# A two-block transformer forward pass: the mLSTM half of the first mixer, its convolution moved behind the projections and its cell written as one step

## What is computed

```python
xc = jax.nn.silu(causal_conv(xm, conv_w, conv_b))          # 4 taps, 1024 features
q = heads(xc, wq); k = heads(xc, wk) * (Dh ** -0.5); v = heads(xm, wv)
dlog = jnp.where(causal, bcum[..., :, None] - bcum[..., None, :] + i_t[..., None, :], -jnp.inf)
m_t = jnp.maximum(bcum + m_prev_b, m_intra)
a_t = jnp.exp(bcum + m_prev_b - m_t)
qk = jnp.einsum('bhcld,bhcsd->bhcls', q, k) * jnp.exp(dlog - m_t[..., None])
num = a_t[..., None] * jnp.einsum('bhcld,cbhde->bhcle', q, c_prev) + jnp.einsum('bhcls,bhcse->bhcle', qk, v)
den = a_t * jnp.einsum('bhcld,cbhd->bhcl', q, n_prev) + jnp.sum(qk, axis=-1)
hid = num / jnp.maximum(jnp.abs(den), jnp.exp(-m_t))[..., None]
hid = head_rms_norm(hid, norm_w, H) * jax.nn.sigmoid(og.astype(F32))
```

## Time and profile before

| | before |
|---|---|
| median of 3 runs | 3710.71 us (3708.18 to 3719.13) |
| the profiled execution | 3716.57 us; its span 3714.8 us |
| PE, PE weight load busy | 81%, 63% of the span |
| DVE, ACT, POOL busy | 66%, 21%, 17% |
| DMA | 858.87 MB, mean 231 GB/s |
| mean granted TensorE clock | 0.899 |

### The profile page before, as it was taken

How to read it: one execution, slowest core, us unless ns; L and a number is a source line. 1 busy time by engine, 2 the same in 40 slices (tenths; PEclk the granted TensorE clock), 3 DMA queues, 4 the chain that set the end, 5 groups by cost and what they waited for, 6 DMA issues and landing times. The chain is left out here.

```text
span 3714.8 us, 45654 instructions
## 1 busy us (share of the span) xinstructions
PE 3005.0 (81%) x17504; PEld 2349.6 (63%) x17504; DVE 2464.5 (66%) x4579; ACT 777.1 (21%) x1927; POOL 633.9 (17%) x520
## 2 busy tenths in 40 slices
PE   7787796778786898677777779977878999975898
PEld 7576693333332598533333339976767999974798
DVE  5342467777777686777677758754446878765686
ACT  1213221222222232222222220012223001013300
POOL 0000003444445100254444520000000000000000
PEclk8899897988889899788988889977998999987999
DMA  6152358999999643799999966633213665640464
GB/s 204 59 169 67 114 166 325 415 411 408 415 410 421 235 136 117 284 415 415 415 406 409 419 286 178 191 103 100 83 35 109 178 190 161 188 151 6 121 182 152
DMA packets 469113, 858.87 MB, mean 231 GB/s; under 512 B 18720, under 2 KB 398496, under 8 KB 402464
## 3 DMA queue, kind: packets, MB, share of 16 engines
q0 software_dynamic: 73728, 536.90, 35.1%
q1 hardware_dynamic: 394880, 318.80, 28.1%
q10 hardware_dynamic: 288, 0.24, 0.0%
HBM read 848.55 MB, written 7.34 MB: 230 GB/s over the span
## 5 line engine op out<-in xcount | busy, mean ns | idle before, releaser
L2136 PE MATMUL banks<-arena,arena 128*128 128x512 f32 x1792 | 939.5, 683 | 344.2 <-ACT arena L2192 343.4
L2136 PEld LDWEIGHTS banks<-arena,arena 128*128 128x128 f32 x1792 | 381.6, 220 | 884.9 <-issue 454.7
L2096 POOL DMA_INDIRECT arena<-in_peer_uv,arena x512 | 628.9, 1228 | 1449.3 <-DVE arena L2278 759.5
L2301 DVE CUSTOM_DVE_ANT_0 arena<-arena,normed 128x1024 f32<-128x1024 f32 x512 | 626.5, 1224 | 260.3 <-DMA arena<-in_peer_uv,arena 258.0
L354 DVE TENSOR_TENSOR weight_ring_part<-weight_ring,weight_high_parts 128x2048 fp32r<-128x2048 f32 (+2 forms) x244 | 539.8, 2212 | 8.4
L2827 PE MATMUL banks<-normed_columns_part,weight_high_parts 128*128 128x256 f32 x1408 | 403.8, 287 | 10.7 <-PEq L302 9.0
L2828 PE MATMUL banks<-normed_part,weight_high_parts 128*128 128x256 f32 x1408 | 401.8, 285 | 0.0
L2829 PE MATMUL banks<-normed_columns_part,weight_ring_part 128*128 128x256 f32 x1408 | 401.8, 285 | 0.0
L663 PE MATMUL banks<-weight_high_parts,arena_part 128*128 128x256 f32 x1216 | 344.4, 283 | 42.5 <-PEq L302 28.9
L351 DVE CAST weight_high_parts<-weight_ring 128x2048 fp32r<-128x2048 f32 (+2 forms) x244 | 289.9, 1188 | 123.1 <-PE banks L665 79.6
L664 PE MATMUL banks<-weight_ring_part,arena_part 128*128 128x256 f32 x1216 | 341.6, 281 | 0.0
(11 more groups left out here) (506 smaller groups left out, 4357.7 us busy)
## 6 DMA issues: line engine op xcount, KB each, us to landing
weight_ring<-in_ffn_w_gate SPq DMA_DIRECT2D x88, 512.0 KB, 4.0
weight_ring<-in_ffn_w_up SPq DMA_DIRECT2D x88, 512.0 KB, 5.3
weight_ring<-in_ev_w_in SPq DMA_DIRECT2D x33, 1024.0 KB, 5.5
weight_ring<-in_ffn_w_down SPq DMA_DIRECT2D x32, 1024.0 KB, 5.3
weight_ring<-in_od_w_in SPq DMA_DIRECT2D x23, 1024.0 KB, 5.4
weight_ring<-in_xa_wkv SPq DMA_DIRECT2D x16, 1024.0 KB, 5.8
weight_ring<-in_peer_wq SPq DMA_DIRECT2D x16, 1024.0 KB, 5.7
weight_ring<-in_ev_w_out SPq DMA_DIRECT2D x12, 1024.0 KB, 5.7
```

Of the source, the lines that this page charges most:

```text
L2096: pool.indirect_dma_start(out=ring[:, slot(i, s), :], out_offset=None, in_=table, in_offset=bass.IndirectOffsetOnAxis(ap=index[:, i % 2, s ...
L2136: mm = pe.matmul(k.ps[:, 2 * b + half, :], diag[:, n % 2, s, :], v, start=h == 0 and g == 0 and s == 0, stop=h == PEER_HEADS - 1 and g == ...
L2301: dve.tensor_tensor_reduce(out=ring[:, here, 0:D], in0=ring[:, here, 0:D], in1=k.xn[:, b, :], scale=1.0, scalar=0.0, op0=ALU.mult, op1=ALU ...
```

## The change

1. `memory_columns` takes further pairs of gain and destination. In the SSD half's convolution step ACT evacuates each bank twice, with the first memory's gain into `memT` and with the second's into `memT_2`. The next step stores `memT_2` to memory (1 MB) and SP waits until it is stored. The second fetch of the memory rows and the second making of columns are gone; `memT` is fetched back (1 MB) during `rows_out`.
2. `zero_front` is an instruction of `columns_out` now. The 4-tap convolution is cut by chunk: chunks 0 and 1 between DVE's evacuations in `columns_out` (each instruction waits for the one before), chunks 2 to 7 between its weight splits in `rows_out`. The convolution step is gone.
3. Everything from Silu to the transposed output columns is one step, `mlstm`'s, with an order written out for each engine. The 32 side units stand at fixed places in PE's stream, `store_side` also feeds the weight ring after each, products run four banks ahead, and spread rows and scores are read by DVE out of PSUM. The sums with `spread` are fewer: `bcum` and the peak are applied as a bias of Exp and to row maxima. The root mean square is taken by ACT's Square for both chunks. Outputs are turned back chunk by chunk (`turn_out`), `finish_side` is gone.
4. The columns are written at once as rounded part `high` (ACT) and rest `low` (DVE, out of the bank), for the SSD half in its `to_columns`, for the mLSTM half in `keep_columns` and `keep_rest`. `split_columns` is gone. The split of the first two `ev_w_out` tiles stands on DVE between `keep_rest(0)` and `keep_rest(1)`.

```diff
+    def memory_columns(self, block, gain, rows, memT, *also):
...
+                for g, dst in ((gain, memT),) + also:
+                    act.activation(dst[:, m, :], self.ps[:, CHAIN + m % SIDE_BANKS, 0:T], ACT.Copy,
+                                   scale=self.col(g, m)).then_inc(self.memory_kept.sem, 1)
...
-    mixT = k.take(16, T)
+    columns = [k.take(16, T) for _ in range(2)]
+    high, low = (k.part_of(c) for c in columns)
...
+    k.conv(padded, "ssd_conv_w", "ssd_conv_b", 12, 4, xbcT, memory=("norm_mem0", memory_rows, memT, ("norm_mem1", memT_2)))
...
+        @block.sync
+        def _(sp):
+            sp.dma_start(k.kept_memory, memT_2).then_inc(k.memory_stored.sem, 16)
+            k.memory_stored.adds(16)
+            sp.wait_ge(k.memory_stored.sem, k.memory_stored.total)
...
-    k.to_columns(y, 8, mixT[:, 0:8, :], "ssd_norm")
...
+    k.to_columns(y, 8, None, "ssd_norm", parts=(high[:, 0:8], low[:, 0:8]))
     k.top = outer
+    mlstm(k, high, low, columns[1][:, 8:12].rearrange("p c t -> p (c t)"), gates, cum[:, :, 16:20], tot[:, :, 16:20], memT)
+    k.land((high, low), 16, "norm_xattn0")
...
-        k.fetch_memory_rows(sp, "mem", memory_rows)
-    zero_front(k, padded, 3)
+    def fetch_memory(sp):
+        sp.dma_start(memT, k.kept_memory).then_inc(k.fetched.sem, 16)
+        k.fetched.adds(16)
...
+    def clear_front(dve):
+        dve.memset(padded[:, :, 0:3], 0.0).then_inc(k.vector_done.sem, 1)
...
+    def convolve(dve, c):
+        for j in range(4):
+            x, w = padded[:, c, j:j + T], k.col("ml_conv_w", j * 8 + c)
+            if j == 0:
+                i = dve.tensor_scalar(xcT[:, c, :], x, w, k.col("ml_conv_b", c), ALU.mult, ALU.add)
+            else:
+                i = dve.scalar_tensor_tensor(xcT[:, c, :], x, w, xcT[:, c, :], ALU.mult, ALU.add)
+            i.then_inc(k.vector_done.sem, 1)
+            dve.wait_ge(k.vector_done.sem, k.vector_done.next())
...
+    def convolve_first(dve, m):
+        if m in (4, 6):
+            dve.wait_ge(k.evacuated.sem, k.evacuated.start + m - 3)
+            convolve(dve, m // 2 - 2)
+    def convolve_rest(dve, j):
+        for c in ((2, 3), (4,), (5,), (6, 7))[j]:
+            convolve(dve, c)
     k.columns_out(k.hT, [512] * 2, lambda e, m, bank: e.tensor_tensor(padded[:, m, 3:], bank, k.wide[:, :], ALU.mult),
-                  also=fetch_heads)
+                  also=fetch_heads, vector_first=clear_front, vector_then=convolve_first)
     k.rows_out(k.hT, [WIDTH] * 4, lambda e, j, b, bank: e.activation(og[:, b, j * WIDTH:(j + 1) * WIDTH], bank, ACT.Sigmoid,
-                                                                     scale=k.rs[:, b:b + 1]))
-    k.conv(padded, "ml_conv_w", "ml_conv_b", 8, 4, xcT, memory=("norm_mem1", memory_rows, memT))
+                                                                     scale=k.rs[:, b:b + 1]),
+               also=fetch_memory, vector_then=convolve_rest)
...
-    with k.step(side=2) as block:
...
+    with k.step() as block:
+        @block.sync
+        def _(sp):
+            k.feed(sp)
+            k.store_side(sp, range(s0, s0 + 16), feed=True)
+            k.feed(sp)
...
+            pe.wait_ge(k.heads_in.sem, k.heads_in.total)
+            for n in range(8):
+                project(n)
+            pe.wait_ge(k.ml_diag.sem, k.ml_diag.start + NB)
+            for b in range(NB):
+                pe.matmul(k.ps[:, 4 + b, :], k.c("ones"), diag[:, b].rearrange("p h s -> p (h s)"), start=True,
+                          stop=True).then_inc(k.ml_spread.sem, 1)
...
+            pe.wait_ge(k.ml_raised.sem, k.ml_raised.start + 8)
+            for n in range(8, 24):
+                project(n)
...
+            pe.wait_ge(k.fetched.sem, k.fetched.total)
+            k.multiply_side(pe, u0, u0 + 4)
...
+            pe.wait_ge(k.ml_kept.sem, k.ml_kept.start + 24)
+            for i in range(2):
+                for c in range(4):
...
+            for b in range(NB):
+                for h in range(H):
+                    for c in range(2):
+                        mm = pe.matmul(score_bank(b)[:, h, :], qT[:, 2 * h + c, b * P:(b + 1) * P], kT[:, 2 * h + c, b * P:(b + 1) * P],
+                                       start=c == 0, stop=c == 1)
...
+            k.multiply_side(pe, u0 + 4, u0 + 10)
...
+                pe.wait_ge(k.ml_weighted.sem, k.ml_weighted.start + b + 1)
+                for h in range(H):
+                    mm = pe.transpose(spread_bank(b)[:, h, :], shares[:, b, h, :], k.c("ident"))
+                mm.then_inc(k.ml_turned.sem, 1)
...
+            pe.wait_ge(k.ml_rows.sem, k.ml_rows.start + 2)
+            pe.wait_ge(k.ml_values.sem, k.ml_values.start + 1)
+            for n in range(8):
+                sums(n)
+                if n == 3:
+                    k.multiply_side(pe, u0 + 10, u0 + 12)
+            pe.wait_ge(k.ml_rows.sem, k.ml_rows.start + 4)
+            for n in range(8, 16):
+                sums(n)
+                if n == 11:
+                    k.multiply_side(pe, u0 + 12, u0 + 14)
+            for n in range(16, 20):
+                sums(n)
+            k.multiply_side(pe, u0 + 14, u0 + 24)
+            turn_out(0)
+            k.multiply_side(pe, u0 + 24, u0 + 32)
+            turn_out(1)
...
+            for c in range(8):
+                act.activation(xcT[:, c, :], xcT[:, c, :], ACT.Silu).then_inc(k.ml_raised.sem, 1)
+            for n in range(20):
+                keep(n)
+            act.wait_ge(k.ml_biased.sem, k.ml_biased.start + 2)
+            act.activation(w_end, w_end, ACT.Exp).then_inc(k.ml_raised.sem, 1)
...
+            k.keep_side(act, range(s0, s0 + 2))
+            keep_rows(0)
+            keep_rows(1)
+            k.keep_side(act, range(s0 + 2, s0 + 5))
+            keep_rows(2)
+            keep_rows(3)
+            for n in range(8):
+                keep_sums(n)
+            k.keep_side(act, range(s0 + 5, s0 + 6))
+            for n in range(8, 16):
+                keep_sums(n)
+            act.activation(k.spare, k.c("ones")[:, 0:1], ACT.Sqrt).then_inc(k.scalar_done.sem, 1)
+            k.keep_side(act, range(s0 + 6, s0 + 7))
+            square(0)
+            take_root(0)
+            k.keep_side(act, range(s0 + 7, s0 + 9))
+            square(1)
+            take_root(1)
+            k.keep_side(act, range(s0 + 9, s0 + 12))
+            keep_columns(0)
+            k.keep_side(act, range(s0 + 12, s0 + 16))
+            keep_columns(1)
...
+            def keep_rest(b):
+                dve.wait_ge(k.ml_high.sem, k.ml_high.start + 8 * (b + 1))
+                for m in range(8):
+                    t = slice(b * P, (b + 1) * P)
+                    dve.scalar_tensor_tensor(low[:, 8 + m, t], column_bank(b, m // 4)[:, m % 4, :], k.col("ml_norm", m),
+                                             high[:, 8 + m, t].bitcast(F32), ALU.mult, ALU.subtract).then_inc(k.columns_split.sem, 1)
...
+            divide(0)
+            mean(0)
+            for h in range(H):
+                dve.wait_ge(k.ml_summed.sem, k.ml_summed.start + 16 + h + 1)
+                dve.wait_ge(k.ml_sums.sem, k.ml_sums.start + 12 + h + 1)
+                step(dve.scalar_tensor_tensor(num[:, 1, h, :], k.ps[:, h, 0:DIM + 1], decay_prev[:, 1, h:h + 1], num[:, 1, h, :],
+                                              ALU.mult, ALU.add))
+            settled()
+            divide(1)
+            gate_out(0)
+            mean(1)
+            gate_out(1)
+            keep_rest(0)
+            while k.splits <= k.taken + 1:
+                k.split_next(dve, k.taken + 2)
+            keep_rest(1)
...
-    k.land(k.split_columns(mixT, k.take(16, T)), 16, "norm_xattn0")
```

More of the change, by code:

```diff
@@ L431, in _ @@
         def _(pe):
[L432 to L448 removed]
+            self.multiply_side(pe, first, last)
@@ L462, in finish_side, with keep_side @@
+    def keep_side(self, act, whole):
+        for s in whole:
+            act.wait_ge(self.side_done.sem, s + 1)
+            if s >= STAGES:
+                act.wait_ge(self.side_stored[s % STAGES].sem, 16 * (s // STAGES))
+            act.activation(self.stage[:, s % STAGES, :], self.ps[:, CHAIN + s % SIDE_BANKS, 0:WIDTH],
+                           ACT.Copy).then_inc(self.side_out.sem, 1)
+            self.side_out.adds(1)
     def finish_side(self):
@@ L1517, in even_mixer, with keep @@
-    with k.step() as block:
+            def keep(n):
+                act.wait_ge(k.ml_projected.sem, k.ml_projected.start + n + 1)
+                bank = k.ps[:, n % 4, 0:T]
+                if n < 8:
+                    act.activation(v_ext[:, n % 2, n // 2, 0:DIM], bank, ACT.Copy).then_inc(k.ml_kept.sem, 1)
+                else:
+                    is_key, m = chunk_of(n)
+                    act.activation((kT if is_key else qT)[:, m, :], bank, ACT.Copy,
+                                   scale=1.0 / 16 if is_key else 1.0).then_inc(k.ml_kept.sem, 1)
@@ L1588, in even_mixer @@
-    with k.step(side=1) as block:
-        @block.tensor
```

(27 more changed lines are left out.)

492 lines of the change are left out of this document (223 added, 269 removed).

## The result

| | before | after |
|---|---|---|
| median, beside each other | 3711.72 us (3708.18 to 3719.13, 4 runs) | 3668.49 us (3659.21 to 3676.47, 4 runs) |
| the profiled execution | 3716.57 us, span 3714.8 | 3664.38 us, span 3662.6 |
| mean granted TensorE clock | 0.899 | 0.905 |

The ratio is 0.9881, with a 95% interval of 0.9865 to 0.9897: faster by 43.2 us of the medians. The forecast was 3667.6 us.

The account below looks back on a forecast made before the run. No engine bounded the stretch; the order of steps did. The cell's 46.9 us less, minus costs of 2.7, 0.8 and 0.3, gave 43.1 us less: a median of 3667.6 us, range 3658 to 3682.

Parts of the forecast that it names:

- the cell: Silu to output columns as one step: 103.7 us to `land`'s first product instead of 150.6, so 46.9 us less.
- the clock rival: Rival, chance 0.04: PE's work in the cell runs at the lower clock level, +96 us over the whole step, 3763 us.
- The products of PE: In the cell: PE's products, priced by the distance of their evacuations, sum to 95.8 us at full clock.
- Ten hand-overs: In the cell: PE waits ten times for 0.15 us at hand-overs between engines, 1.5 us in all.
- Silu's wait: Start of the cell: the fifth v product waits for ACT's first kept bank, 0 to 1.2 us, taken as 1.0.
- The tail: Behind the cell's last transpose, uncovered: ACT's 8 copies 2.4 us, DVE's 8 rests 2.3 us, 0.1 us of hand-over.
- What was to be paid: Costs outside the cell: SSD half's `to_columns` +2.7 us, convolution in `columns_out` +0.8 us, in `rows_out` nothing.
- Second gain: SSD half's convolution step: 8 more copies on ACT end just behind DVE's taps, +0.3 us (0 to 0.5).
- The marks that were named: Signs in the changed kernel's profile, among them the first product of `columns_out` near 237.
- Hand-overs don't hide: Rival, chance 0.12: longer-held sums and changes between engines make the cell 15 us longer, 3683 us.
- The convolution isn't hidden: Rival, chance 0.04: at 2.4 us a chunk and more, `rows_out` gets longer by up to 4 us, 3672 us.
- The claim that `land` stays cold: Start of `land`: clock unchanged because PE is idle for 5.2 us before it; staying up would win some 2 us.

Follow-up runs that it names:

- e3: e2 with four of ACT's eight Silu chunks alternated with the first four kept banks: 3662.89 us, ratio 0.9864.
- e7: Changed kernel with all 32 side units in one run behind the projections instead of six portions: 3678.32 us, ratio 0.9925.
- e8: Changed kernel with three convolution chunks instead of two in the first tile of `rows_out`, one less in `columns_out`: 3662.18 us, one execution.
- e12: The changed kernel again, unaltered, on the same chip as e11: 3662.04 us, ratio 0.9882.
- e4: Kernel before with only the column halves changed (both `to_columns` write rounded part and rest, no `split_columns`): ratio 0.999.
- e6: Changed kernel with the convolution in a step of its own again: 3682.43 us, ratio 0.9931.
- e1: The changed kernel again, unaltered, beside e2 to e4: 3668.11 us, ratio 0.9877.
- e2: Changed kernel with the transposes of the outputs moved before the last side products: 3665.71 us, ratio 0.9872.
- e9: e3 with the SSD half's second split moved into `columns_out` and no fetch behind SP's last store: 3658.23 us, ratio 0.9859.
- e11: The kernel of e9 again, on a second chip: 3653.64 us, ratio 0.9871.
- e10: The changed kernel again, unaltered, on the same chip as e9: 3664.67 us, ratio 0.9874.

## Why the prediction was right, and where it was right by offset

**The total.** 43.1 us were forecast, 43.2 measured between the medians. That they agree to 0.1 is luck, since the ratio's interval reaches from 38 to 50 us. In the stretch it was less exact: -46.9 + 2.7 + 0.8 = -43.4 forecast, -45.4 measured, and another 0.3 forecast ahead of it. Two errors partly cancel there: the cell was 2.8 us shorter than forecast, and `columns_out` 1.1 us longer. (The chance of "faster" was also added up wrong: all but the clock rival, and half of that one, are 0.98 and not 0.96.)

**The products of PE: right.** The last transpose ends at 380.72 + 1.04 = 381.76; from 285.62 that is 96.14, less the wait of 0.44: 95.7 us against 95.8. Term by term it holds too, if less closely: the side products took 55.3 us (55.3 said), the sums 10.4 (10.4), q and k 13.8 (13.8), the scores 3.6 (3.8), the transposes 3.7 (3.9), v 7.25 without its wait (6.9). A single price can be read in e3, where no wait falls among the eight v products: 289.82 - 282.84 = 6.98 us, priced at 8 x 0.863 = 6.90. Pricing a product by the distance of its evacuations, in a stretch where PE doesn't wait, needs no model of the engine and was good to 0.4 us a term here and to 0.1 us in the sum.

**The waits: all too dear.** Ten hand-overs at 0.15 us, 1.5 us in all, measured nothing: PE's three idle lines above leave no room for one of that size. The portions of side work are longer than what each had to hide, and e7 shows that it is this, not that hand-overs are free. Silu's wait was taken at 1.0 us and is 0.44. The first bank was kept earlier, since ACT's lines are

```profile
285.58 1.28 ACT L1753 ACT_TABLE_LOAD   x1 [0.29 <-PEq L324]
286.87 2.56 ACT L1753 ACTIVATE arena<-arena 128x256 f32<-128x256 f32 x8
289.34 1.18 ACT L1714 ACTIVATE arena<-banks 128x256 f32<-128x256 f32 x4
```

and eight chunks take 2.56 us, between the 1.9 and 3.2 of the earlier trace rows; I took the upper end because the row was nearer by form. And Silu does need a table of its own. It starts 1.29 us after the load does: the drain that the Trainium skill adds to each switch ("ScalarE: Activation LUTs", section "What ACT_TABLE_LOAD costs") isn't seen here either, and the wait that would have been 1.4 us longer by it was shorter than forecast.

**The tail: right in kind, 0.5 us too long.** ACT 2.17 us, then DVE 2.16, said were 2.4 and 2.3; the change of step 0.3, said 0.4:

```profile
381.79 2.17 ACT L1750 ACTIVATE arena_part<-banks,feature_columns 128x128 fp32r<-128x128 f32 x8 [0.49 <-PE banks L1649]
...
384.00 2.16 DVE L1835 SCALAR_TENSOR_TENSOR arena_part<-banks,feature_columns,arena_part 128x128 fp32r<-128x128 f32 x8 [5.61 <-ACT arena_part L1750]
```

DVE's first rest waits for ACT's eighth copy, as foreseen. Together: hand-overs 1.5, Silu 0.56, tail and change 0.48, start 0.16, products 0.1 make 2.8 us, and the cell was 101.2 us where 104.0 was forecast from the same mark.

**What was to be paid.** `to_columns`: 2.5 us, said 2.7. `rows_out`: nothing, said nothing, and e8 put the point where it would cost at the place that the forecast named. The chunk itself was 1.97 us in the forecast; in the trace a chunk runs from 272.53 to 274.54 with the start of the next instruction:

```profile
272.53 0.41 DVE L1558 TENSOR_SCALAR arena<-arena,feature_columns 128x256 f32<-128x256 f32 x1
272.98 1.53 DVE L1560 SCALAR_TENSOR_TENSOR arena<-arena,feature_columns,arena 128x256 f32<-128x256 f32 x3
274.54 1.23 DVE L373 CAST weight_high_parts<-weight_ring 128x2048 fp32r<-128x2048 f32 x1
```

`columns_out` cost 1.9 us, said 0.8. Its own mechanism was right: the first of the two chunks costs nothing, since PE runs ahead, and the second moves the end, PE's idle time behind it going from 0.84 to 1.54 us: 0.7. The other 1.1 had no term in the sum. It is the clock in its first ten microseconds, here before, after and in e12:

```profile
234.20:244.20 10.00, 9.91 (x70) 9.94 (x71) 2.74 (x4) 0.00 (x0) 0.00 (x0) 0.82 0.89 283
```

```profile
233.90:243.90 10.00, 9.90 (x60) 9.93 (x61) 1.68 (x4) 0.00 (x0) 0.00 (x0) 0.69 0.93 282
```

```profile
238.30:248.30 10.00, 10.00 (x70) 10.00 (x71) 2.89 (x5) 0.00 (x0) 0.00 (x0) 0.82 0.92 288
```

Ten fewer products at 0.69 than at 0.82. PE is idle for 8.6 us ahead of it, 2.5 longer than before, and I had costed that idle time at its length alone. But the longer idle time isn't shown to be the cause. e12 is the same program with the same 10.47 us ahead, and its `columns_out` cost 0.8 us (26.36), as forecast; e3's took 26.32. With still more idle time ahead, 9.26 us, and no convolution in it, `columns_out` ran at 0.83 in e4 (25.55) and at 0.69 in e6 (26.78). The three profiles with 27.5 began within 0.25 us of each other (223.53 to 223.76), and in them the last 16 side matmuls ahead of `to_columns` already took 5.2 to 5.3 us, where e12 and e6 have 3.69. What decides between 26.3 and 27.5 is open.

**Second gain: nothing, said 0.3.** With two copies for each bank ACT's last ends before DVE's last tap, which is at 105.87 (its last copy ends at 105.69):

```profile
105.22 0.47 ACT L530 ACTIVATE arena<-banks,feature_columns 128x256 f32<-128x256 f32 x1
```

Within a group the copies start 0.36 to 0.38 us apart, not 0.43 as I took from the earlier trace rows. The 1 MB store landed in 3.9 us, under Silu and the first side product, and cost nothing.

**The marks that were named.** "The first product of `columns_out` near 237" came at 234.00. The term behind it was right (10.47 us from the first split; 7.98 + 2.7 = 10.7 was said); the whole stretch had begun 2.8 us earlier. An absolute time in a profile was a poor thing to forecast, and a distance between two marks would have been a good one.

**The rivals.** *Hand-overs don't hide* is out for this order of the step, and e7 shows that it is the order: with other places for the same products the cell is 14 us longer, close to the 15 that the rival named, though by long waits in two places (and cold transposes behind them) and not by a short one at each sum. *The convolution isn't hidden* is out, by half a microsecond a tile. *The clock stays down* is out: 1.00 over the 96.2 us. The rule on short idle times in "TensorE: Matmul & The Clock Gate" (section "A second HAM failure mode: psum-queue depth-cycling", the Trainium skill) had little to bite on, since PE had but one such time in the cell. The claim that `land` stays cold was right (0.70 over its first 5.6 us). What a warm one would give was said as 2 us: it was 0.9 against a start at 0.88 (e3 to e1, e2 to e6), and 2.7 against e12's start at 0.79 (e9's 95.06 to its 97.74).

## What to carry to other kernels

Where a chain of small steps leaves one engine after another alone, price the joined step by that engine's work alone and test each wait against the length of independent work that stands ahead of it; put that work in portions where the chain turns from one engine to another, and keep the last portion for behind the chain's last product. Then look at which engine ends the step, the one that only issues transfers included. Compare kernels by distances between marks inside the changed stretch: of 52 us between two profiles here 7 lay outside it. And take more than one profile: `columns_out` of one program took 26.4 and 27.5 us.

## What the runs showed of the hardware that was not expected

- The same instructions behind the stretch took from 3168 to 3186 us in the profiles of these kernels, measured from the mark of the cross attention stage to the end of the span, and not in the order of anything that was changed.
- Idle PE can cost a second time. 1.2 to 1.7 us ahead of `land` left the clock at 1.00 over the next 14 us in four profiles (e2, e3, e9, e11). 4.7 us gave 0.88 in four (the changed kernel, e1, e10, e6), 0.81 in e8 and 0.79 in e12. 13.9 us ahead of the cell gave 0.76 in the window of 4 us that begins 1.7 us behind its first product. But equal idle times didn't give equal clocks: 8.6 us ahead of `columns_out` were followed by 0.69 to 0.82, 9.3 us by 0.69 and 0.83. So the second price can be bounded (0 to 3 us here), not forecast.
- An SP instruction that issues a transfer takes 0.34 to 0.43 us and counts when SP ends the step: one of them less brought `land` 0.5 us forward.
